# A decoder step on one core: cached keys, values and decays gathered by row number, eight (values: four) consecutive rows of a page to a partition

## The chip, the core and the metric

The kernel runs on one core of one Trainium2 chip. The metric is the device time of one execution in microseconds (us). The text calls the engines PE (TensorE), DVE (VectorE), ACT (ScalarE), POOL (GpSimd) and SP (SyncE). SP computes nothing here; it issues most of the DMAs.

## What is computed

One step of a one-layer decoder: 256 prompt tokens and 8 samples of one token each go through a projection, two kinds of attention beside each other, a gated merge and a mixture of 32 experts. The samples attend to 1024 cached rows each, which lie in 8 pages of 128 rows. Cut to the part that the change touches (all numbers are float32):

```
# cache_k, cache_v (1, 80, 128, 8, 64), cache_logf (1, 80, 128, 8), page_table (8, 8) int32
k_past = cache_k[0][page_table]          # (8 samples, 1024 rows, 8 heads, 64), v_past likewise
suffix = cumsum(logf_past, axis=1, reverse=True) - logf_past      # decays of all later rows
s = einsum('bqhd,bshd->bhqs', q, k_all) * 64 ** -0.5 + cum_new[query] + suffix[key]
o = einsum('bhqs,bshd->bqhd', softmax(s), v_all)
# later: x = x + gate1 * (mix of both attentions) @ w_o;  x = x + gate2 * moe(norm(x))
# moe: top 4 of 32 experts, w_gu (32, 1024, 2048), w_d (32, 1024, 1024)
```

## The kernel before

The program is written out by hand, engine by engine, with semaphores between them. Its first part (about a quarter of the time) holds the projections of the input, the attention of the prompt and of the samples, and the merge. Its second part goes through the experts, four at a time.

**The ring.** Weights, keys and values pass through six slots of 2 MB each. A table (`RING`) lists the items in order of loading, each with its slot: `ada0` to `ada11` (modulation weights), `qa ka va fqk vb rb ga0 ga1 gb0 gb1` (columns of the input projection), `K0` to `K7` (the keys of one sample each), `V0` to `V7` (values), `state`, `wb`, `wo`. SP walks through the table and, for each item, waits until the item before it in that slot has been used. The experts' weights follow, over the same slots and some more homes.

**Keys and values.** An item `K` or `V` is loaded page by page: 128 rows of a page lie on the 128 partitions, 2 KB each, and one DMA of 256 KB brings one page (`load_pages`). The page's number is read from `pages_row` into a register first. SP issues the first four pages of an item, POOL the last four (`second_half`). `K0` holds the eight pages of sample 0, and so on; `V0` holds two pages each of samples 0 to 3, `V1` the next two, and so on, `V4` to `V7` the same for samples 4 to 7.

**Keys on DVE.** `keys_half(b, part)` multiplies four pages of keys by the sample's query, which is the same on every partition, and reduces over the 64 features. The 16 calls stand in DVE's program among the small work of the prompt. The queries of samples 0 and 1 reach all partitions through PE and ACT. Those of samples 2 to 7 go from `q_rows` to DRAM (`q_dram`) and back as three broadcasts (`q_all1` to `q_all3`), all on POOL's queue.

**Decays.** One gather (`lf_rows`) brings the 64 pages' decays with one page on a partition. PE turns them with eight transposes (`past_lf`). A product with ones gives the sum of each page (`page_sums`), a product with a strict triangle the suffix inside a page (`in_page_suffix`). DVE adds up the later pages and gets `past_bias`.

**The prompt's attention.** It runs over the steps s = 0 to 10 on PE, with one head behind another: `pair_scores` fills two banks for two heads, DVE masks (`head_mask`) and normalizes (`head_norm`), ACT takes the exponentials, PE turns the probabilities (`head_turn`) and multiplies by the values (`head_values`). Among these stand tiles of the gates, modulation weights, and `cached_values(i)`: eight products of the samples' probabilities with the item `V{i}`. A bank is used again when DVE has taken what it held (`vector_bank`). A slot is free again when `release` says so.

Of the kernel before, what the change touches and what calls it, by code (L numbers as in the profile page):

```python
# [26 lines left out]
I32 = mybir.dt.int32  # L27
U32 = mybir.dt.uint32
# [15 lines left out]
PAGES, PAGE, N_PHYS = 8, 128, 80  # L44
NE, TOPK, FF = 32, 4, 1024
# [49 lines left out]
def decoder_step(nc, x_prompt, x_sample, c_prompt, c_sample, cache_k, cache_v, cache_logf, state_gla,  # L95
# [4 lines left out]
    with ExitStack() as ctx:  # L100
# [21 lines left out]
        pages_row = sb("pages_row", [1, NS * PAGES], I32)  # L122
        pages_col = sb("pages_col", [NS * PAGES, 1], I32)
# [48 lines left out]
        past_lf = tok[:, 0, 0:512].rearrange("p (a j) -> p a j", j=PAGES)  # L172
# [33 lines left out]
        lf_rows = gla_S[0:NS * PAGES, :, :, :].rearrange("p a b c -> p (a b c)")  # L206
# [52 lines left out]
        q_shift = dec_max[:, 0:36].rearrange("p (i c) -> p i c", c=9)  # L259
        dec_diag = tiny(HA * NS, HA * NS)  # L260
        dec_inv = tiny(P, HA, NS)
# [64 lines left out]
        for item in ITEMS:  # L326
            s = SLOT_OF[item]
            slot_count[s] += 16 * (PAGES // 2 if item[0] in "KV" else 2 if item in WIN else 1)
            landing[item] = (s, slot_count[s])
# [10 lines left out]
        def arrived(eng, item):  # L340
            eng.wait_ge(landed[landing[item][0]], landing[item][1])
# [18 lines left out]
        def page_of(item, n):  # L360

            i = int(item[1:])
            return (i, n) if item[0] == "K" else (4 * (i // 4) + n % 4, 2 * (i % 4) + n // 4)

        def second_half_landed(item):

            i = int(item[1:])
            again = i >= 4 and item != "K7"
            return sig(f"second_half_{item[0]}{i - 4 if again else i}"), 16 * (PAGES // 2) * (2 if again else 1)

        def load_pages(eng, item, half, done, slot_free):

            slot = landing[item][0]
            rows = (cache_k if item[0] == "K" else cache_v)[0].rearrange("n s h d -> n s (h d)")
            order = range(half * PAGES // 2, (half + 1) * PAGES // 2)
            at_ = [b * PAGES + j for b, j in (page_of(item, n) for n in order)]
            pages = [eng.value_load(pages_row[0:1, a:a + 1], min_val=0, max_val=N_PHYS - 1) for a in at_]
            eng.wait_ge(*slot_free)
            for j, page in zip(order, pages):
                eng.dma_start(ring[:, slot, j * WA:(j + 1) * WA],  # L380
# [2300 lines left out]
```

## Time and profile before

| | us |
|---|---|
| median of 3 runs | 1247.59 |
| lowest and highest | 1246.07, 1248.51 |
| span of the profiled execution | 1245.7 |
| PE busy in it | 1167.0 |
| DVE busy | 335.1 |
| ACT busy | 174.9 |
| POOL busy | 48.3 |

The profile shows one execution, from its first instruction to its last; its own time is this span of 1245.7 us, and the median of the runs is 1.9 us above it. In it 500.76 MB were moved at a mean of 402 GB/s. Busy shares are means over parts of the program with different limits, so what matters is read stretch by stretch: which engine is full there, and what ended the waits of the engine that carries the end. Rows of the timeline give start, duration, engine, line, operation and tiles, and in brackets how long the engine had been idle and what released it.

### The profile page before, as it was taken

Reading aid. Unit: us, or ns where it says so; the run is one execution under the profiler, and the core shown is the slowest. Engines: PE = TensorE matmul, PEld = TensorE weight load, DVE = VectorE, ACT = ScalarE, POOL = GpSimd, SP = SyncE. Lnnn points to the kernel's source line nnn. Section 1 sums busy time; section 2 is a strip of 40 time slices with the busy share of each in tenths; the row PEclk is TensorE's granted clock in tenths of the full one; section 3 lists DMA queues with packets and bytes.
Section 4 is the critical chain, followed back from the end, with each engine's and each line's share of the span. In section 5 each row is a group of like instructions: output and inputs, shape, how many; then the busy total and the mean of one; then the engine's idle time right before and its main releaser. Section 6 shows DMA issues by size and latency. Waiting matters only on the chain.

```text
span 1245.7 us, 15295 instructions
## 1 busy us (share of the span) xinstructions
PE 1167.0 (94%) x6044; PEld 587.2 (47%) x6044; DVE 335.1 (27%) x688; ACT 174.9 (14%) x346; POOL 48.3 (4%) x95
## 2 busy tenths in 40 slices
PE   6999999999999999989899979998989989899997
PEld 4788756688543442424243435344332424243333
DVE  3389975523221030111101111111021011103123
ACT  3133232100211100200020011002000200020102
POOL 1132122000000000000000000000000000000000
PEclk9999999999999999999999998999999999999999
DMA  9998999998799999999999999999999999999995
GB/s 341 357 388 314 379 347 383 404 408 345 292 407 429 428 428 427 427 429 428 429 429 417 428 428 411 429 427 428 428 428 427 428 427 429 429 427 427 422 417 204
DMA packets 72700, 500.76 MB, mean 402 GB/s; under 512 B 9049, under 2 KB 11171, under 8 KB 43836
## 3 DMA queue, kind: packets, MB, share of 16 engines
q1 hardware_dynamic: 65840, 478.38, 93.2%
q0 software_dynamic: 6576, 21.42, 4.7%
q8 instruction: 42, 0.69, 0.2%
q14 instruction: 22, 0.18, 0.0%
q10 hardware_dynamic: 220, 0.09, 0.0%
HBM read 496.48 MB, written 3.38 MB: 401 GB/s over the span
## 4 chain that ended last, share of the span: by engine, by line
PE 66%; DMA 25%; SPq 4%; ACT 2%; DVE 2%; issue 2%; DVEq 0%
PE ps L1076 22%; DMA ring<-in_w_d 16%; PE ps L1163 11%; PE ps L518 11%; DMA early<-in_w_d 8%; PE ps L1260 4%; PE ps L1017 4%; PE ps L862 2%; PE ps L927 2%; SPq L2526 2%; PE ps L423 2%; PE ps L960 1%; DMA ring<-in_w_ada 1%; PE ps L475 1%; SPq L2410 1%
## 5 line engine op out<-in xcount | busy, mean ns | idle before, releaser
L1076 PE MATMUL ps<-ring,zone 128*64 128x512 f32 x1488 | 414.9, 593 | 6.0 <-DMA ring<-in_w_gu 3.4
L1163 PE MATMUL ps<-ring,oT 128*64 128x512 f32 x784 | 239.5, 620 | 28.9 <-DMA ring<-in_w_d 15.1
L1076 PEld LDWEIGHTS ps<-ring,zone 128*64 128x64 f32 x1488 | 132.3, 137 | 220.6 <-issue 217.5
L518 PE MATMUL ps<-early,ring 128*128 128x264 f32 x640 | 149.0, 389 | 1.8 <-DVE early L1735 1.4
L2189 DVE TENSOR_SCALAR zone<-ps 128x1024 f32<-128x1024 f32 x14 | 17.1, 1225 | 480.2 <-PE ps L1076 457.8
L1163 PEld LDWEIGHTS ps<-ring,oT 128*64 128x64 f32 x784 | 73.2, 142 | 149.8 <-issue 129.6
L518 PEld LDWEIGHTS ps<-early,ring 128*128 128x128 f32 x640 | 119.5, 190 | 30.2 <-issue 8.9
L1076 PE MATMUL ps<-zone 128*64 128x512 f32 x284 | 114.9, 594 | 2.1 <-DMA ring<-in_w_gu 2.1
L1076 PE MATMUL ps<-early,zone 128*64 128x512 f32 x240 | 98.8, 593 | 0.0
L1547 ACT ACTIVATE ps<-zone 128x1024 f32<-128x1024 f32 x14 | 14.4, 1027 | 452.7 <-DVE zone L2189 452.7
L1076 PEld LDWEIGHTS ps<-zone 128*64 128x64 f32 x284 | 35.2, 137 | 77.7 <-issue 73.8
L2201 DVE TENSOR_TENSOR dec_scores<-dec_scores,ps 128x8 f32<-128x8 f32 x80 | 12.9, 162 | 209.8 <-PE ps L1260 113.4
L1163 PE MATMUL ps<-zone,oT 128*64 128x512 f32 x112 | 52.8, 627 | 11.6 <-DMA ring<-in_w_d 11.6
L1163 PE MATMUL ps<-early,oT 128*64 128x512 f32 x128 | 61.5, 637 | 0.0
L1017 PE MATMUL ps<-zone,early 128*128 128x224 f32 x224 | 44.2, 355 | 0.1
L1017 PEld LDWEIGHTS ps<-zone,early 128*128 128x128 f32 x224 | 41.8, 190 | 0.5
L423 PE MATMUL ps<-ident,zone 128*128 128x128 f32 (+4 forms) x214 | 35.1, 288 | 3.9 <-ACT oT L1570 3.9
L423 PEld LDWEIGHTS ps<-ident,zone 128*128 128x128 f32 (+4 forms) x214 | 26.4, 178 | 25.4 <-issue 20.3
L2202 DVE SCALAR_TENSOR_TENSOR xT<-ps,modT,xT 128x256 f32<-128x256 f32 x80 | 38.1, 478 | 0.0
L1163 PEld LDWEIGHTS ps<-zone,oT 128*64 128x64 f32 x112 | 15.5, 144 | 46.9 <-issue 35.1
L1767 DVE TENSOR_REDUCE dec_scores<-ring 128x32 f32<-128x2048 f32 x16 | 36.6, 2288 | 0.6
L1260 PE MATMUL ps<-zone,gla_S 128*128 128x264 f32 x112 | 33.9, 390 | 1.2 <-ACT oT L1570 0.6
(408 smaller groups left out, 978.8 us busy)
## 6 DMA issues: line engine op xcount, KB each, us to landing
ring<-in_w_gu SPq DMA_DIRECT2D x93, 2048.0 KB, 27.0
ring<-in_w_d SPq DMA_DIRECT2D x45, 2048.0 KB, 22.4
zone<-in_w_gu SPq DMA_DIRECT2D x16, 2048.0 KB, 25.3
early<-in_w_gu SPq DMA_DIRECT2D x15, 2048.0 KB, 30.0
ring<-in_w_ada SPq DMA_DIRECT2D x12, 2048.0 KB, 13.1
ring<-in_w_in SPq DMA_DIRECT2D x18, 1024.0 KB, 12.2
early<-in_w_d SPq DMA_DIRECT2D x8, 2048.0 KB, 24.8
zone<-in_w_d SPq DMA_DIRECT2D x7, 2048.0 KB, 19.5
```

Of the source, the lines that this page charges most:

```text
L423: return pe.transpose(out, in_, ident[0:n, 0:n])
L518: ins = pe.matmul(bank[0:width, 0:T], w[:, k, c0:c0 + width], hT[:, k, :], start=(k == 0), stop=(k == KT - 1))
L862: ins = pe.matmul(bank[:, 0:T], wb[n][:, k, m * P:(m + 1) * P], (oT[:, :, :], obT)[n][:, k, :], start=(k == 0), stop=(k == 3))
L927: ins = pe.matmul(bank[:, 0:T], wo[m // 4][:, k, feature_columns(m % 4)], hT[:, k, :], start=(k == 0), stop=(k == KT - 1))
L1017: ins = pe.matmul(bank[:, kk * 4 * PCAP:(kk + 1) * 4 * PCAP], tok[:, t, k * P:(k + 1) * P], pick[:, t, :, :].rearrange("p e s -> p (e s)") ...
L1076: ins = pe.matmul(ps[64 * j:64 * j + CAP, c, :], xg[:, k, 2 * par + j, :], rows, start=False, stop=(k == KT - 1), skip_group_check=True)
L1163: ins = pe.matmul(ps[64 * j:64 * j + CAP, 4 + c, :], hidT[:, k, j * CAP:(j + 1) * CAP], w[j][:, kk, c * 512:(c + 1) * 512], start=(k == 0) ...
L1260: ins = pe.matmul(ps[:, 6 + m % 2, 0:T], ye_tok[par][:, feature_columns(m)], putT[:, par, :], start=(par == pars[0]), stop=(par == 1))
L1767: V.tensor_reduce(dec_scores[:, b:HA * NS:NS, part_no * n:(part_no + 1) * n] .rearrange("p h j -> p j h"), kc.rearrange("p j (h d) -> p j ...
L2189: V.tensor_scalar(hid, sig_ps, LIMIT, None, ALU.min).then_inc(sig("gate_ready"), 1)
L2202: return V.scalar_tensor_tensor(out=xT[:, m, 0:TP], in0=bank[:, 0:TP], scalar=modT[:, 40 + m, 0:1], in1=xT[:, m, 0:TP], op0=ALU.mult, op1= ...
L2526: sp.dma_start(places[slot][:, kk * D:(kk + 1) * D], dn_last[2 * (PAIRS - 1) + j, 2 * s_ + kk // 2, :, kk % 2, :])\
```

## The change

Rows are addressed by number. A page has 128 rows, so eight consecutive rows of a page lie on one partition: partition p holds rows 8r to 8r + 7 of page j, with j = p // 16 and r = p % 16. The numbers are computed on the chip: a product of the page numbers with a 0/1 matrix on PE, and three small operations on DVE. POOL then issues the gathers: eight for the decays, one of 2 MB for each `K`, two of 1 MB for each `V` (a `V` item now holds four consecutive rows for each of two samples). SP loads no keys and no values any more, and the register reads are gone.

`K0` now waits for the second half of `qa` (`qa_second`) where POOL's half of it waited for `ka`. The other gathers stand where the second halves stood in POOL's program.

With eight consecutive rows on a partition, the suffix inside a partition is added up first on DVE (six adds), and one product with the triangle over the 64 totals gives the rest (`later_rows`). The transposes and the two products over 512 columns go.

`cached_values(i)` takes two items at once, 16 products, each time the four samples after each other. The calls stand at other places: `V0` and `V1` in step 6 where they stood in steps 5 and at the head of 6; `V2` and `V3` in step 8 where they stood in 7 and 8; `V4` and `V5` behind the first part of the linear attention's states; `V6` and `V7` before its third head.

```
-        pages_row = sb("pages_row", [1, NS * PAGES], I32)
-        pages_col = sb("pages_col", [NS * PAGES, 1], I32)
+        rows_at = sb("rows_at", [P, NS], I32)
+        half_rows_at = sb("half_rows_at", [P, 2, NS], I32)
...
-        lf_rows = gla_S[0:NS * PAGES, :, :, :].rearrange("p a b c -> p (a b c)")
+        lf_rows = gla_S[:, :, :, :].rearrange("p a b c -> p (a b c)")[:, 0:NS * RUN * HA]
+        page_of_row = part(attn_flat, slice(0, PAGES), 1024, P)
...
+            pe.wait_ge(sig("row_numbers"), 3)
+            pe.wait_ge(sig("page_rows"), 1)
+            bank = vector_bank()
+            vector_filled(pe.matmul(bank[:, 0:NS], page_of_row, pages_f, start=True, stop=True), "rows_at")
...
-            pe.wait_ge(sig("lf_rows"), 16)
-            bank = vector_bank()
-            for h in range(HA):
-                ins = transpose(bank[:, h * 64:(h + 1) * 64], lf_rows[:, h:h + HA * (PAGE - 1) + 1:HA])
-            vector_filled(ins, "past_lf")
...
+            pe.wait_ge(sig("lf_total"), 1)
             bank = vector_bank()
-            vector_filled(pe.matmul(bank[:, :], ones[:, :], past_lf.rearrange("p a b -> p (a b)"),
-                                    start=True, stop=True), "page_sums")
-            tiles("fqk", 256, "kb", [1])
-            bank = vector_bank()
-            vector_filled(pe.matmul(bank[:, :], after[:, :], past_lf.rearrange("p a b -> p (a b)"),
-                                    start=True, stop=True), "in_page_suffix")
+            vector_filled(pe.matmul(bank[:, 0:HA * NS], after[:, :], lf_total, start=True, stop=True), "later_rows")
...
             def cached_values(i):
-                item, group = f"V{i}", i // 4
-                arrived(pe, item)
-                pe.wait_ge(*second_half_landed(item))
+                items, group = (f"V{i}", f"V{i + 1}"), i // 4
+                for item in items:
+                    arrived(pe, item)
...
-                if s == 6:
-                    cached_values(1)
...
-                elif s in (5, 7, 8):
-                    cached_values(s - 5)
+                elif s in (6, 8):
+                    cached_values(s - 6)
...
-                cached_values(4 + i)
-            cached_values(6)
+                if i == 0:
+                    cached_values(4)
...
                 if h == 2:
-                    cached_values(7)
+                    cached_values(6)
...
+            dve.wait_ge(sig("lf_rows"), 16 * NS)
+            by_head = past_suffix.rearrange("p (h b) j -> p h b j", b=NS)
+            lf = lf_rows.rearrange("p (b j h) -> p h b j", b=NS, h=HA)
+            V.memset(past_suffix[:, :, RUN - 1], 0.0)
+            chain(V.tensor_copy(by_head[:, :, :, RUN - 2], lf[:, :, :, RUN - 1]))
+            for j in range(RUN - 3, -1, -1):
+                chain(V.tensor_tensor(by_head[:, :, :, j], by_head[:, :, :, j + 1], lf[:, :, :, j + 1], ALU.add))
...
+            pool.wait_ge(sig("page_rows"), 3)
+            for b in range(NS):
+                gather_rows(lf_rows[:, b * RUN * HA:(b + 1) * RUN * HA], lf_runs, rows_at[:, b:b + 1], sig("lf_rows"))
...
+                pool.wait_ge(*freed[slot_before(f"K{b}")])
+                gather_rows(ring[:, s, :], k_runs, rows_at[:, b:b + 1], gathered(f"K{b}")[0])
...
-            arrived(pool, "ka")
-            second_half("K0")
+            pool.wait_ge(sig("qa_second"), 32)
+            load_keys(0)
             pool.wait_ge(vector_free, v_index["q_rows"])
             nc.gpsimd.dma_start(q_dram, q_rows).then_inc(sig("q_stored"), 16)
             pool.wait_ge(sig("q_stored"), 16)
...
             for b in range(1, NS):
-                second_half(f"K{b}")
+                load_keys(b)
```

POOL's program before, from the first gather on (L2605 the decays, L380 the second half of `K0`, L2615 and L2618 the queries out and back; the ISA rows set registers):

```order
L2605 DMA gla_S<-in_cache_logf,pages_col 64x1024
L377 TENSOR_LOAD pages_row
...
L380 DMA ring<-in_cache_k 128x512
L380 ISA
L380 DMA ring<-in_cache_k 128x512
L2615 DMA q_dram<-zone 8x512
L2618 DMA early<-q_dram 128x1024 x2
L2618 DMA oT<-q_dram 128x1024
L377 TENSOR_LOAD pages_row
```

And POOL's program after the change, at the same place (L2604 is every gather: decays, keys, values):

```order
L2604 DMA gla_S<-in_cache_logf,rows_at 128x64 x8
L2604 DMA ring<-in_cache_k,rows_at 128x4096
L2630 DMA q_dram<-zone 8x512
L2633 DMA early<-q_dram 128x1024 x2
L2633 DMA oT<-q_dram 128x1024
L2604 DMA ring<-in_cache_k,rows_at 128x4096 x7
L2638 DMA vb_dram<-rows 8x512
L2604 DMA ring<-in_cache_v,half_rows_at 128x2048 x8
```

All of `K1` now stands behind the queries' way to DRAM and back, and eight gathers stand ahead of `K0`.

PE's program before, in steps 5 and 6 (L742 the samples' sums, L712 the cached values, L423 turning probabilities, L688 to L690 values of the prompt, L662 and L666 the scores of heads 6 and 7):

```order
L742 MATMUL ps<-dec_scores,ones 128x512
L712 MATMUL ps<-ring,dec_scores 8x512 x8
L423 MATMUL ps<-ident,attn 128x128 x3
...
L690 MATMUL ps<-attn,v_tok 64x128
L712 MATMUL ps<-ring,dec_scores 8x512 x8
L662 MATMUL ps<-zone 128x128 x2
L666 MATMUL ps<-early,ident 128x128 x2
L662 MATMUL ps<-zone 128x256 x2
L666 MATMUL ps<-early,ident 128x256 x2
L423 MATMUL ps<-ident,attn 128x128 x3
```

And after the change (L732, L703, L418, L680, L652 and L656 are the same lines of code in this order):

```order
L732 MATMUL ps<-dec_scores,ones 128x512
L418 MATMUL ps<-ident,attn 128x128 x3
...
L680 MATMUL ps<-attn,v_tok 64x128
L652 MATMUL ps<-zone 128x128 x2
L656 MATMUL ps<-early,ident 128x128 x2
L652 MATMUL ps<-zone 128x256 x2
L656 MATMUL ps<-early,ident 128x256 x2
L703 MATMUL ps<-ring,dec_scores 8x512 x16
L418 MATMUL ps<-ident,attn 128x128 x3
```

Both sets of eight products, which stood ahead of the scores of heads 6 and 7, now stand behind them.

## Rows read from the trace of the kernel before

**Rows 1.** The page: span, and busy time of TensorE.

```profile
span 1245.7 us, 15295 instructions
...
PE 1167.0 (94%) x6044; PEld 587.2 (47%) x6044; DVE 335.1 (27%) x688; ACT 174.9 (14%) x346; POOL 48.3 (4%) x95
```

**Rows 2.** Stretches: length, busy us of PE, PEld, DVE, ACT, POOL; clock, DMA share, GB/s.

```profile
330.00:340.00 10.00, 10.00 (x50) 3.41 (x48) 0.00 (x0) 0.00 (x0) 0.00 (x0) 1.00 0.70 274
...
400.00:1200.00 800.00, 742.06 (x3531) 307.58 (x3529) 116.32 (x250) 76.73 (x143) 0.50 (x1) 0.98 1.01 426
```

**Rows 3.** The chain that ended last, in the experts: start, us, what.

```profile
599.72 26.74 DMA ring<-in_w_d
```

**Rows 4.** Timeline of DVE, among the keys.

```profile
66.08 2.27 DVE L1766 TENSOR_TENSOR ring<-ring,early 128x2048 f32<-128x2048 f32 x1
...
76.05 2.29 DVE L1766 TENSOR_TENSOR ring<-ring,early 128x2048 f32<-128x2048 f32 x1 [1.13 <-DMA ring<-in_cache_k]
...
82.02 0.71 DVE L1811 TENSOR_TENSOR zone<-zone 128x528 f32<-128x528 f32 x1 [1.35 <-ACT zone L1353]
...
90.49 0.68 DVE L1860 COPY early<-ps 128x512 f32<-128x512 f32 x1
...
102.08 1.83 DVE L1875 TENSOR_TENSOR early<-early 128x64 f32<-128x64 f32 x6
```

**Rows 5.** Timelines of DVE and PE at the first probabilities of the prompt.

```profile
153.05 0.35 DVE L1927 TENSOR_SCALAR attn<-attn,small 128x256 f32<-128x256 f32 x1
...
153.55 0.55 PE L423 MATMUL ps<-ident,attn 128*128 128x128 f32 x3
```

**Rows 6.** Timeline of PE: the decays' transposes and first product.

```profile
81.14 1.09 PE L423 MATMUL ps<-ident,gla_S 64*128 64x64 f32 x8
...
95.85 1.02 PE L631 MATMUL ps<-early,ones 128*128 128x512 f32 x2
```

**Rows 7.** Timeline of POOL: the gather of decays, the first two broadcasts.

```profile
10.90 1.10 POOL L2605 DMA_INDIRECT gla_S<-in_cache_logf,pages_col  x1 [7.77 <-DMA pages_col<-in_page_table]
...
61.87 1.08 POOL L2618 DMA_DIRECT2D early<-q_dram  x2 [5.55 <-DMA q_dram<-zone]
```

**Rows 8.** DMA queues: 65 to 80 us (two rows), then q0, 65 to 67.9.

```profile
q0 software_dynamic: 1076, 3.68, 64.2%
q1 hardware_dynamic: 1117, 2.13, 38.7%
...
q0 software_dynamic: 300, 1.11, 98.4%
```

**Rows 9.** Timelines of PE and SP up to ka; DMA views: issue to landing.

```profile
17.66 0.58 PE L423 MATMUL ps<-ident,zone 36*128 36x36 f32 x3
...
19.39 1.41 SPq L2399 DMA_DIRECT2D ring<-in_w_ada  x1
...
ring<-in_w_ada SPq DMA_DIRECT2D x1, 2048.0 KB, 17.0
...
36.94 1.93 PE L450 MATMUL ps<-ring,early 128*32 128x256 f32 x32
...
22.31 4.89 SPq L2415 DMA_DIRECT2D ring<-in_w_in  x1
...
ring<-in_w_in SPq DMA_DIRECT2D x1, 1024.0 KB, 19.5
...
44.65 2.05 PE L518 MATMUL ps<-early,ring 128*128 128x264 f32 x8
```

**Rows 10.** Timelines of DVE and PE in the prompt's attention and behind it.

```profile
165.17 0.35 DVE L1912 SCALAR_TENSOR_TENSOR attn<-ps,f_tok,early 128x128 f32<-128x128 f32 x1 [1.08 <-PE ps L666]
...
168.26 1.91 PE L712 MATMUL ps<-ring,dec_scores 128*8 128x512 f32 x16
...
174.43 0.49 PE L662 MATMUL ps<-zone 64*128 64x128 f32 x4 [0.86 <-DVE small L1962]
...
204.28 1.09 PE L799 MATMUL ps<-early 64*64 64x128 f32 x16 [0.93 <-DVE gla_S L2003]
```

More of the change, by code:

```diff
@@ L340, in arrived @@
         def arrived(eng, item):
-            eng.wait_ge(landed[landing[item][0]], landing[item][1])
+            eng.wait_ge(*(gathered(item) if item[0] in "KV" else (landed[landing[item][0]], landing[item][1])))
         def gate_up_done(n, first, gone):
@@ L358, in expert_load, with gathered, values_in @@
             return q * 24 + at_, slot, (q * 3 + (at_ // PLACES + 1)) * 16 + slot_count[slot]
-        def page_of(item, n):
-            i = int(item[1:])
[L363 to L380, printed above, removed]
-                              rows[bass.ds(page, 1), :, :].rearrange("a s c -> (a s) c")).then_inc(done, 16)
+        def gathered(item):
+            s, _ = landing[item]
+            before_ = [other for other in ITEMS[:ITEMS.index(item) + 1] if other[0] in "KV" and landing[other][0] == s]
+            return sig(f"gathered{s}"), sum(16 if other[0] == "K" else 32 for other in before_)
+        def values_in(item):
+            i = int(item[1:])
+            return [4 * (i // 4) + 2 * (i % 2) + n for n in range(2)], (i % 4) // 2
         block = ctx.enter_context(nc.Block())
@@ L1324, in _ @@
             dma(c_rows[1:9, :], c_sample, "c_rows")
+            with nc.allow_non_contiguous_dma(reason="64 page numbers"):
+                dma(pages_sb[:, :], page_table.rearrange("b j -> j b"), "pages")
             vectors = {"b_ada": b_ada, "g_mix": g_mix, "g_ffn": g_ffn, "g_gla": g_gla, "b_alpha": b_alpha}
@@ L2387, in load @@
                 earlier = slot_before(item)
-                if item[0] not in "KV" and earlier is not None:
+                if item[0] in "KV":
+                    return
+                if earlier is not None:
                     sp.wait_ge(*freed[earlier])
@@ L2614, in _, with load_values @@
+            def load_values(i):
+                s, _ = landing[f"V{i}"]
+                samples, half = values_in(f"V{i}")
+                pool.wait_ge(*freed[slot_before(f"V{i}")])
+                for n, b in enumerate(samples):
+                    gather_rows(ring[:, s, n * 2048:(n + 1) * 2048], v_runs, half_rows_at[:, half, b:b + 1],
+                                gathered(f"V{i}")[0])
+            pool.wait_ge(sig("qa_second"), 32)
+            load_keys(0)
             pool.wait_ge(vector_free, v_index["q_rows"])
```

97 lines of the change are left out of this document (53 added, 44 removed).

## The prediction

> **What bounds the kernel now.** I read the page first. The span is 1245.7 us and TensorE (PE) is busy for 94% of it [rows 1]. Then I read stretches of the span for who is full. From 400 to 1200 us the DMA engines are full (share 1.01, 426 GB/s) while PE is busy for only 742 of 800 us [rows 2], and the chain shows why: PE stands until a slice of w_d, issued when its slot came free, has landed 26.74 us later [rows 3]. So the last 900 us are DMA-bound. But this DMA stream does not start full. Between 330 and 340 us the engines are only 0.70 busy with PE at 10.00 of 10 us [rows 2]: every slot holds a weight, and the stream waits for PE to use one. So the end is the moment at which PE reaches the experts, plus a stretch that the change doesn't touch. A microsecond won or lost by PE before 330 us is one won or lost at the end; one won by the DMA alone before that is lost in the gap at 330.
>
> The change lies before 220 us. There PE is nearly always busy, and its partner is VectorE (DVE), which works through 16 half samples of keys: per half a multiply of 2.27 us and a reduction that is about as long [rows 4]. The reader is to see in rows 4 that this queue has almost no slack from 66 us on: it waits 1.13 us for the second half of K1 and 1.35 us for ScalarE. All of it stands before the prompt's attention. At the first probabilities DVE ends at 153.40 and PE turns them at 153.55 [rows 5]: 0.15 us of slack. So a late DVE is passed on to PE, and an early PE alone gains little.
>
> **What it removes.** PE loses the eight transposes of the decays (1.09 us) and two products over 512 columns (1.02 us as shown for one) [rows 6], and gets two small ones: some 2.5 us off PE. DVE loses two copies (0.68 each), the add and the second add over 512 elements (about the same each), keeps six adds (1.83) and gets one pass over 512 elements and four small operations: 4.5 us become about 3.3, 1.2 off [rows 4].
>
> **K1 comes late.** Before, half of K1 was issued by SP, ahead of DVE's need, and only the other half by GpSimd. Now all keys are on GpSimd's queue, and K1 stands behind the wait for the stored queries and behind three broadcasts. The first two are issued at 61.87 [rows 7], the third right behind them; the queue then has 3 x 0.52 + 2.10 = 3.67 MB to move before K1 is complete. Bounds: alone on the engines this queue moved 1.11 MB in 2.9 us, 383 GB/s, which gives 9.6 us, so 74 us at the earliest; with the vb weights beside it, it moved just 3.68 MB from 65 to 80 us [rows 8], so 79.5 us. I take 77, between them: vb is still loaded beside it, but SP's K2 half is not. DVE asks for K1 at 66.08, so it stands 10.9 us in place of the 1.13 it stood in the middle of K1; the 1.35 us wait for ScalarE is swallowed, and 1.2 us of work is gone: 10.9 - 1.1 - 1.35 - 1.2 = 7.3 us late (bounds 4.3 and 9.8). What is queued behind: the products and the decay of the prompt, which PE asks for later and gets in time, and the sum over decays, for which PE will stand some us near the place of its 95.85 product [rows 6]; PE then still arrives before DVE at the first probabilities. K2 to K7 are ahead of their use: their slots are free one sample (9.1 us of DVE) earlier than they are needed.
>
> **K0 comes too early.** It now waits for the second half of qa, which SP issues ahead of ada3, and not for ka. Ahead of it are eight gathers of decays. The one gather in the trace took GpSimd 1.10 us for 64 rows [rows 7]. The row numbers come from a product that stands ahead of PE's 17.66 transposes [rows 9]; eight gathers from some 19 us on end at 28 us at the earliest. So K0's 2.10 MB (5.4 us at 389 GB/s) go out beside ada3, issued 19.39 and landed 17.0 us later at 36.4, which PE reads at 36.94, and beside ka, issued 22.31 and landed 19.5 us later at 41.8, which PE reads at 44.65 [rows 9]. ka moves to 47.2, 2.6 us after PE's need; ada3 by 0 to 5 us, by when K0 starts. Bounds 0 (gathers so slow that K0 goes behind ka) and 5.4; I take 2.6. q_rows, and with it K1, moves by the same.
>
> How the queues share matters here. From 65 to 80 us GpSimd's queue had 64.2% of the engines' time and SP's 38.7% [rows 8], each with small packets. The Trainium skill (DMA: Bandwidth & Descriptors, Queues, rings and completion order) says that an engine goes round-robin between its queues packet by packet; larger packets in the gathers would then give them more than that, K1 nearer to 74 and ada3 later. The two nearly cancel, and the trace has no gather of such rows; the sum stays with the shares of the rows.
>
> **The values move behind a wait.** V0 stood in step 5 and V1 at the head of step 6, each 1.91 us of PE (3.7 for both, as neighbours overlap a little); behind them PE stood 0.86 us until DVE released a bank for the next scores at 174.43. DVE got there along its own chain: from 165.17, where it had waited 1.08 us for PE, it did not stand for PE again [rows 10]. Now both stand behind those scores. The wait grows by 3.7 us, and from 174.43 to 190 PE has no other wait in which the 3.7 us could be done. So +3.7 us. Bounds: 0, if DVE were also earlier there by as much; 3.7. I take 3.7. Later V5 moves to before the wait of 0.93 us at 204.28 [rows 10] and fills it: -0.9.
>
> **Sum.** DVE late 7.3, K0 2.6, slack at 153.5 us -0.15, values +3.7 - 0.9 = +12.5 us. PE's own 2.5 us are not in it: PE waits for DVE there. 1245.7 + 12.5 = 1258.2 for an execution like the profiled one; the median of the runs (1247.59) is 1.9 above that span, so 1260. With the low bounds of K1 and K0: 4.3 + 0 - 0.15 + 2.8 = +6.9, 1254.5. With the high ones: 9.8 + 5.4 + 2.65 = +17.8, 1265.5.
>
> **Rivals.**
> 1. As above, 1254.5 to 1265.5: 0.58.
> 2. Only the values cost (1250): K1 lands by 70 us, which needs its 3.67 MB in 6 us, more than any stretch of the trace moved, or DVE's order hides it. 0.12.
> 3. Faster, and the mechanism is the DMA. The caches are 33.5 MB. At the 389 GB/s of 65 to 80 us they take 86.2 us, at the 426 GB/s of the experts' stretch 78.7 [rows 2, 8]; the 7.5 us come off the end if up to 330 us PE is paced by landings: 1240. Against it: the gap at 330 us, and that PE's waits in rows 5 and 10 are for DVE. It decides if PE's stands for landings before 330 us are over 7 us. 0.08. The Trainium skill (DMA: Bandwidth & Descriptors, Measured) speaks for this one: it asks for DMAs of 1 MiB or more, with 341 GB/s at 1 MB and 425 at 16 MB, and the old pieces are 256 KB. By that rule alone the change should be a gain.
> 4. No measurable change (1245 to 1250): PE's 2.5 us come through because K1 is early, and the values' wait shrinks with it. 0.07.
> 5. Much slower (1266 to 1280): a gather of 128 rows costs GpSimd several times 1.10 us or blocks while its queue drains. V4 to V7 are eight gathers, and between PE's work near 174.43, behind which the first of their slots comes free, and its use of values next to 204.28 lie 30 us [rows 10]. It decides from some 4 us a gather; at 5 they last 40 us, 10 us more: 1270. 0.15.
>
> **How the numbers follow.** A measurement of this kernel tells about 0.2% (2.5 us) from no change. Faster is case 3 and the lower edge of case 4: 0.10. Same is the rest of case 4 and a third of case 2: 0.09. Slower is the rest: 0.81. The range 1249 to 1266 leaves out case 3, most of case 4 and case 5 above 1266: a little over 2 in 10 at most. Case 1's own range is 1254.5 to 1265.5.
>
> **What would show it.** In the changed kernel's timeline of DVE: a wait of some 11 us for K1 ahead of the third multiply of keys (it starts near 79 us), the keys finished some 9 us later than before, and no other wait for keys. On PE: a wait for ada3 or ka before 50 us, of 2 to 5 us in all; a wait for the sum over decays near 100 us; a wait of some 4.5 us ahead of the scores of heads 6 and 7. The DMA gap before the experts is there and wider. The prediction is wrong if K1 lands before 72 us, if K0's start lies behind ka's landing, if a gather occupies GpSimd for 3 us or more, or if the experts start at the same time as before.

## The result and the profile after

The changed kernel takes 1260.02 us (median of 4 runs, 1258.69 to 1261.86), the kernel before 1248.03 us in the same comparison (4 runs, 1246.07 to 1248.51). The ratio is 1.0101, 95% interval 1.0079 to 1.0124: slower by 1%, which is 12.6 us by the ratio and 12.0 by the two medians. The profiled execution of the changed kernel has a span of 1256.9 us, 11.2 above that of [rows 1].

The page of the changed kernel: span, busy time, queues, and the chain that ended last.

```profile
span 1256.9 us, 14539 instructions
PE 1169.6 (93%) x6036; PEld 589.5 (47%) x6036; DVE 334.2 (27%) x693; ACT 174.8 (14%) x346; POOL 49.7 (4%) x65
...
q1 hardware_dynamic: 56624, 461.60, 88.6%
q0 software_dynamic: 5088, 38.19, 7.7%
...
PE 59%; DMA 27%; DVE 7%; issue 3%; SPq 2%; ACT 2%; POOL 0%; DVEq 0%
```

The last line is the chain; in the kernel before it reads:

```profile
PE 66%; DMA 25%; SPq 4%; ACT 2%; DVE 2%; issue 2%; DVEq 0%
```

The reader is to see that the busy times hardly say "slower". No engine has more than 3 us more to do than in [rows 1], and there are 756 instructions fewer. Only the chain gives a hint: DVE carries 7% of it and carried 2% before. What changed is when things arrive, so the timelines have to be read.

The changed kernel's timeline of GpSimd (start, us, instruction, idle before and its releaser), from the decays to the third gather of keys:

```profile
19.32 1.15 POOL L2604 DMA_INDIRECT gla_S<-in_cache_logf,rows_at  x1 [15.62 <-DVE half_rows_at L1704]
...
28.30 0.94 POOL L2604 DMA_INDIRECT gla_S<-in_cache_logf,rows_at  x1 [0.30 <-issue]
29.55 0.94 POOL L2604 DMA_INDIRECT ring<-in_cache_k,rows_at  x1 [0.30 <-issue]
```

Most gathers of 128 rows cost GpSimd 0.94 us, whether a row is one of decays or one of keys (16 KB); single ones in this timeline took longer, up to 2.74 us (at 107.17 us). K0 goes out at 29.55 us, as forecast. Its 2 MB run beside ada3, and PE waits for ada3. The changed kernel's timeline of PE in the opening:

```profile
19.70 3.39 PE L445 MATMUL ps<-ring,early 128*32 128x256 f32 x32
...
40.86 3.42 PE L445 MATMUL ps<-ring,early 128*32 128x256 f32 x32 [2.39 <-DMA ring<-in_w_ada]
```

Two things stand in the second row: the wait for ada3 (2.39 us), and 3.42 us for 32 matmuls that took 1.93 before [rows 9]. The granted clock explains the second. Stretches of the changed kernel (columns as in [rows 2]):

```profile
36.00:40.00 4.00, 2.46 (x12) 1.75 (x10) 0.00 (x0) 0.39 (x1) 0.00 (x0) 1.00 1.00 416
40.60:43.80 3.20, 2.94 (x28) 1.38 (x32) 0.00 (x0) 0.00 (x0) 0.00 (x0) 0.50 1.05 388
...
160.20:166.60 6.40, 6.09 (x25) 4.42 (x26) 4.35 (x17) 2.02 (x8) 0.08 (x1) 0.50 1.01 422
...
184.00:187.20 3.20, 3.02 (x20) 2.25 (x24) 1.69 (x7) 0.00 (x0) 1.21 (x2) 0.50 0.02 7
```

A clock of 0.50 is the 1.2 GHz level. It stands right behind each of the three longer waits of PE (2.39, 2.72 and 4.16 us). Up to 350 us the kernel before has one such stretch (3.4 us, at 323 us), the changed one has four, of 17 us in all (at 20.0, 40.5, 160.0 and 183.9 us). The first of these four, and the one of the kernel before, stand behind no wait.

The changed kernel's timeline of DVE at K1 and at the last keys; the first is the multiply that stands at 66.08 in [rows 4], where it had no wait:

```profile
77.53 2.29 DVE L1763 TENSOR_TENSOR ring<-ring,early 128x2048 f32<-128x2048 f32 x1 [5.98 <-DMA ring<-in_cache_k,rows_at]
...
151.59 2.29 DVE L1764 TENSOR_REDUCE dec_scores<-ring 128x32 f32<-128x2048 f32 x1
```

And the changed kernel's timeline of PE at the sum over decays, the first probabilities, and the scores of heads 6 and 7 (the last two answer to the rows at 153.55 and 174.43 in [rows 5, 10]):

```profile
103.90 0.33 PE L626 MATMUL ps<-small,after 128*128 128x64 f32 x2
...
160.51 0.90 PE L418 MATMUL ps<-ident,attn 128*128 128x128 f32 x3 [2.72 <-DVE attn L1923]
...
184.18 0.80 PE L652 MATMUL ps<-zone 64*128 64x128 f32 x4 [4.16 <-DVE small L1958]
```

Two stretches of the changed kernel: the DMA gap before the experts (its place has moved with PE by one slice), and the experts.

```profile
340.00:350.00 10.00, 10.00 (x51) 3.61 (x51) 0.00 (x0) 1.73 (x5) 0.00 (x0) 1.00 0.74 276
...
400.00:1200.00 800.00, 742.04 (x3543) 308.92 (x3541) 118.11 (x243) 78.75 (x146) 0.50 (x1) 0.98 1.01 427
```

**Where the time goes.** I read in both traces when PE starts at the same places of the program. The table is my own, worked out from the start times.

| PE starts | before | after | later by |
|---|---|---|---|
| the product behind ada3 (q's shift) | 42.79 | 48.19 | 5.4 |
| scores of heads 0, 1 | 146.32 | 149.46 | 3.1 |
| scores of heads 2, 3 (behind the first probabilities) | 154.19 | 161.35 | 7.2 |
| scores of heads 6, 7 | 174.43 | 184.18 | 9.8 |
| the transposes behind the attention | 190.72 | 204.97 | 14.3 |
| the new rows, behind the last values | 223.19 | 236.95 | 13.8 |
| the experts | 328.29 | 340.42 | 12.1 |

So there are three places: the opening (+5.4), the first probabilities (+4.0) with a stretch at 1.2 GHz behind them (+2.6), and the values behind the scores (+4.5). Between the first two PE's own saving shows (-2.3). The values' wait of 4.16 us stands ahead of the scores of heads 6 and 7, but two sets of products left the same stretch, so the two cancel there; the cost shows one row further down, where the products now stand.

How much of this is the clock can be read off the same rows. The matmuls in the four stretches took 1.46, 1.49, 2.8 and 1.35 us more than the same ones before, 7.1 in all, and the stretch at 323 us had cost the kernel before 1.6. So about 5.5 of the 12.1 us are the clock, and 6.6 are waits and work.

### The profile page after: what moved, and what is told of

It reads as the page before. It is cut to its first block, busy times and chain, and to the rows that moved or that the text cites. A ratio compares the mean times of both kernels' runs of the same rounds, so it can differ in the third digit from the quotient of the medians.

```text
span 1256.9 us, 14539 instructions
## 1 busy us (share of the span) xinstructions
PE 1169.6 (93%) x6036; PEld 589.5 (47%) x6036; DVE 334.2 (27%) x693; ACT 174.8 (14%) x346; POOL 49.7 (4%) x65
## 4 chain that ended last, share of the span: by engine, by line
PE 59%; DMA 27%; DVE 7%; issue 3%; SPq 2%; ACT 2%; POOL 0%; DVEq 0%
PE ps L1066 23%; DMA ring<-in_w_d 16%; PE ps L1153 11%; DMA early<-in_w_d 8%; PE ps L517 4%; PE ps L1250 4%; PE ps L1007 4%; DVE ring L1763 3%; PE ps L852 2%; PE ps L917 2%; DMA ring<-in_w_ada 2%; DVE dec_scores L1764 1%; PE ps L418 1%; PE ps L950 1%; SPq L2407 1%
## 5 line engine op out<-in xcount | busy, mean ns | idle before, releaser
L2185 DVE TENSOR_SCALAR zone<-ps 128x1024 f32<-128x1024 f32 x14 | 17.1, 1224 | 479.4 <-PE ps L1066 457.0
L418 PE MATMUL ps<-ident,zone 128*128 128x128 f32 (+4 forms) x214 | 35.1, 288 | 3.9 <-ACT oT L1560 3.9
L418 PEld LDWEIGHTS ps<-ident,zone 128*128 128x128 f32 (+4 forms) x214 | 26.4, 178 | 24.8 <-issue 19.8
## 6 DMA issues: line engine op xcount, KB each, us to landing
ring<-in_w_ada SPq DMA_DIRECT2D x12, 2048.0 KB, 13.8
ring<-in_w_in SPq DMA_DIRECT2D x18, 1024.0 KB, 11.8
zone<-in_w_d SPq DMA_DIRECT2D x7, 2048.0 KB, 19.5
```

The costliest lines, as they stand in the source:

```text
L418: return pe.transpose(out, in_, ident[0:n, 0:n])
L2185: V.tensor_scalar(hid, sig_ps, LIMIT, None, ALU.min).then_inc(sig("gate_ready"), 1)
```

## The experiments

Each kernel ran in 5 rounds beside the kernel before. Ratios are those to the kernel before, with the 95% interval. Experiments 1 to 4 ran on one chip, 5 to 7 on a second, 8 and 9 on a third, 10 and 11 on a fourth. The reading of experiments 5 to 11 needs this.

**1. Values back ahead of the scores.** In the loop over steps s of the attention of the changed kernel, with the second group left behind them:

```diff
+                if s == 6:
+                    cached_values(0)
...
-                elif s in (6, 8):
-                    cached_values(s - 6)
+                elif s == 8:
+                    cached_values(2)
```

Each call works through two loads of values, so the first call is V0 and V1.

> The changed kernel, but both V0 and V1 are multiplied ahead of the scores of heads 6 and 7 (where V1 stood before the change). Theory 1 (PE waits there for DVE, and the values only fill the wait): the wait of 4.16 us shrinks to under 1 us, its stretch at half clock goes with it, and the end comes 3.7 to 4.5 us earlier than with the whole change: 1255.5 to 1256.5 us, 1.006 to 1.0068 of before. Theory 2 (the time went to the DMA queues, or to the form of the products, four samples after each other): the place does not matter, 1260 us, 1.010.

1254.2 us (1248.39 to 1259.5), ratio 1.0053 (1.0036 to 1.0069): 5.8 us below the changed kernel. The kernel's timeline of PE at the scores of heads 6 and 7:

```profile
180.53 0.49 PE L652 MATMUL ps<-zone 64*128 64x128 f32 x4 [0.61 <-DVE small L1960]
```

The wait of 4.16 us is 0.61, and the four matmuls take 0.49 us, not 0.80: the stretch at 1.2 GHz is gone with the wait. The size is less sure than the mechanism: the 12 runs spread over 11 us, the profiled one took 1250.68, and it differs from the changed kernel in more than this place. The wait for ada3 was 4.32 us in it, with 6.8 us at 1.2 GHz, and behind the first probabilities (a wait of 1.95 us) the clock did not fall.

**2. K0 behind ka again.**

```diff
-            pool.wait_ge(sig("qa_second"), 32)
+            arrived(pool, "ka")
             load_keys(0)
```

> The changed kernel, but the gather of K0 waits for ka, as the old second half did, and not for the second half of qa. Theory 1 (K0 beside ada3 costs PE a wait of 2.39 us and 1.5 us of half clock): no wait for ada3, ada3 and ka land before 37 and 43 us, q_rows 4 us earlier, K1 lands near 73.5 in place of 77.5 us, and the end comes some 4 us earlier: 1256 us, 1.0065. Theory 2 (the small gathers of decays ahead of K0 slow ada3, not K0): ada3 still lands at 39 us or later, and the end moves by under 1 us.

1257.0 us (1255.56 to 1258.71), ratio 1.0076 (1.0058 to 1.0094). No wait for ada3 is left, and PE reaches the product behind it at 44.34 us, 3.9 us earlier, although the stretch at 20 us is there too. The interval overlaps that of the changed kernel, so it is the trace and not the ratio that shows this gain. DVE's wait for K1 is still there (timeline of DVE, then of PE at the first probabilities):

```profile
72.83 2.29 DVE L1763 TENSOR_TENSOR ring<-ring,early 128x2048 f32<-128x2048 f32 x1 [5.13 <-DMA ring<-in_cache_k,rows_at]
```

```profile
155.81 0.55 PE L418 MATMUL ps<-ident,attn 128*128 128x128 f32 x3 [2.72 <-DVE attn L1923]
```

**3. K1 right behind K0, ahead of the wait for the queries.** On top of experiment 2:

```diff
             load_keys(0)
+            load_keys(1)
             pool.wait_ge(vector_free, v_index["q_rows"])
...
-            for b in range(1, NS):
+            for b in range(2, NS):
                 load_keys(b)
```

> As the kernel with K0 behind ka, and K1 gathered right behind K0, ahead of the wait for the queries. Theory 1 (K1 behind the queries' way to DRAM and back makes DVE late, and DVE passes that on to PE at the first probabilities): DVE's wait of 5.98 us for K1 is gone, the keys are finished at 146 us or earlier in place of 153.9, PE's wait of 2.72 us for the first probabilities is under 1 us, and the end comes another 5 to 6 us earlier than with K0 behind ka alone: 1250 to 1251 us, 1.002. Theory 2 (K1 only looks late because DVE is free; PE sets the time up to 150 us): the end moves by under 1.5 us against that kernel.

1250.71 us (1248.92 to 1257.85), ratio 1.0037 (1.0022 to 1.0052). DVE no longer waits for K1; it waits 2.57 us for ScalarE where it waited 1.35 before [rows 4], and ends its keys at 144.99 us, 1.9 us earlier than the kernel before. PE's wait at the first probabilities is 0.33 us. The wait at the scores of heads 6 and 7 is untouched (timeline of PE):

```profile
151.53 0.55 PE L418 MATMUL ps<-ident,attn 128*128 128x128 f32 x3 [0.33 <-DVE attn L1923]
...
172.51 0.49 PE L652 MATMUL ps<-zone 64*128 64x128 f32 x4 [4.16 <-DVE small L1958]
```

**4. The kernel before, with its values at the changed kernel's places.** Nothing else of the change.

```diff
-                if s == 6:
-                    cached_values(1)
...
-                elif s in (5, 7, 8):
+                elif s in (6, 8):
+                    cached_values(s - 6)
                     cached_values(s - 5)
...
-                cached_values(4 + i)
-            cached_values(6)
+                if i == 0:
+                    cached_values(4)
+                    cached_values(5)
...
+                    cached_values(6)
```

> The kernel before, with page loads and all, only the products with the values stand at the changed kernel's places: items V0 and V1 behind the scores of heads 6 and 7, V2 and V3 together in step 8, V4 and V5 behind the first part of the states, V6 and V7 before the third head. Theory 1: PE waits 3.7 us longer ahead of those scores (0.86 becomes 4.5), gets 0.9 back later and loses up to 1.7 us at half clock: 1251 to 1252.5 us, 1.0025 to 1.0035. Theory 2 (place doesn't matter): 1248, 1.000.

1253.44 us (1252.83 to 1253.95), ratio 1.0047 (1.0031 to 1.0063), about 5.9 us for one move in the order of PE's work, some more than expected. The timeline of PE has the same wait as the changed kernel, in a kernel without any gather of keys (behind it 6.8 us at 1.2 GHz, and 3.4 more from 224.6 us on):

```profile
174.31 0.80 PE L662 MATMUL ps<-zone 64*128 64x128 f32 x4 [4.16 <-DVE small L1963]
```

**5. Experiments 1 and 3 together.**

> The changed kernel with K0 behind ka, K1 gathered right behind K0, and V0 and V1 multiplied ahead of the scores of heads 6 and 7. Theory 1 (the three places carry the whole loss, each in its own way, and they add up): PE's waits for DVE ahead of the first probabilities and of the scores are under 1 us each; against the kernel with the first two alone (1250.7) the 4 to 5 us of the values come off: 1246 to 1247.5 us, 0.9985 to 0.9995 of before. Theory 2 (a part of the loss lies in the gathers themselves, by their traffic or by GpSimd): it stays above 1249.5 us, 1.0015 or more.

A miss: 1251.28 us (1249.91 to 1253.79), ratio 1.0033 (1.002 to 1.0047). The waits at the probabilities and at the scores are small, as expected (0.35 and 0.61 us). But this execution lost 4.9 us against experiment 3 in the opening. The timelines of ScalarE and of PE there, and a stretch:

```profile
23.94 0.38 ACT L1368 ACTIVATE rows<-ps 128x256 f32<-128x256 f32 x1 [9.61 <-remote]
```

```profile
24.37 0.70 PE L418 MATMUL ps<-ident,rows 128*128 128x128 f32 x2 [2.38 <-ACT rows L1368]
```

```profile
24.40:31.00 6.60, 5.20 (x12) 3.82 (x13) 1.97 (x7) 1.71 (x4) 4.02 (x5) 0.50 1.03 387
```

PE had ended the product that ScalarE copies at 21.99 us, and ScalarE started 1.95 us after it. "remote" means that the trace can't say what released it. Behind that wait PE runs at 1.2 GHz for 6.8 us.

**6. Other DVE work put into the wait for K1.** In the changed kernel the three steps behind the first half of K1 (the new products and the decay of the prompt) go ahead of it:

```diff
-            keys_half(1, 0)
...
+            keys_half(1, 0)
```

> The changed kernel, only DVE's order differs: the products of the new keys and the decay's first part (4.2 us of work) stand ahead of K1's first half and not behind it. Theory 1 (DVE's queue is what carries K1's delay): that work runs inside the wait for K1, the keys are finished some 4 us earlier (near 150 us), PE's wait for the first probabilities (2.72 us) goes, and the end comes 3 to 5 us earlier: 1255 to 1257 us, 1.006 to 1.0075. Theory 2 (PE's late start of 5.4 us, from ada3, sets the time, and DVE hides behind it): under 1 us earlier, since PE's own start is unchanged.

A miss as well: 1263.89 us (1259.8 to 1265.26), ratio 1.0137 (1.0121 to 1.0154). The moved work waits itself, 3.39 us for PE and 1.22 us for ScalarE, because it uses what PE only then makes; the last keys are reduced from 150.75 us, only 0.84 earlier. And the opening had the same late copy (ScalarE at 24.74 us) with 6.8 us at 1.2 GHz, so this time can't be put down to the moved work alone.

**7. The kernel before with 2.1 MB more to move.** GpSimd's queue copies 2.1 MB of keys inside DRAM near 221 us.

```diff
+            nc.gpsimd.dma_start(extra_dram, cache_k[0, 0:8].rearrange("n s h d -> (n s) (h d)"))\
+                .then_inc(sig("extra"), 16)
```

> The kernel before, with one DMA more: GpSimd copies 2.1 MB of keys to an unused place in DRAM near 221 us, when the DMA engines are full and before the gap at 330 us. Theory 1 (the DMA stream has slack before 330 us; there it waits for PE): the gap gets smaller by about the 5.4 us that 2.1 MB take at 389 GB/s, and the time stays within 1 us of before, 0.999 to 1.001. Theory 2 (bytes before 330 us count at the end, so fewer or cheaper ones would be a gain): 5 us slower, 1.004.

1247.98 us (1244.71 to 1251.64), ratio 1.001 (0.9999 to 1.0022), as expected. Two stretches of the kernel with the extra copy, and then one of them in the kernel before:

```profile
310.00:320.00 10.00, 10.00 (x77) 8.40 (x80) 4.80 (x26) 3.67 (x7) 0.00 (x0) 1.00 0.75 293
330.00:340.00 10.00, 10.00 (x50) 3.34 (x48) 0.00 (x0) 0.00 (x0) 0.00 (x0) 1.00 0.85 339
```

```profile
310.00:320.00 10.00, 10.00 (x77) 8.27 (x79) 4.98 (x27) 3.84 (x7) 0.00 (x0) 1.00 0.49 188
```

The extra traffic fills the gap before the experts (0.49 to 0.75, and 0.70 [rows 2] to 0.85) and costs 0.22% at the upper end of the interval. So DMA time that the gathers save or cost before 330 us is worth next to nothing here by itself.

**8 and 9. The decays' gathers behind K0 and K1.** They are the one burst on GpSimd's queue during the late copy of experiment 5. Experiment 8 is experiment 5 with this edit, experiment 9 is experiment 3 with it:

```diff
-            for b in range(NS):
-                gather_rows(lf_rows[:, b * RUN * HA:(b + 1) * RUN * HA], lf_runs, rows_at[:, b:b + 1], sig("lf_rows"))
...
             load_keys(0)
             load_keys(1)
+            for b in range(NS):
+                gather_rows(lf_rows[:, b * RUN * HA:(b + 1) * RUN * HA], lf_runs, rows_at[:, b:b + 1], sig("lf_rows"))
```

> The kernel with all three (the first two gathers of keys back to back behind the arrival of ka, both first gathers of values ahead of the scores), and the eight gathers of the decays moved behind those two gathers of keys, to about 44 us; nothing else. Before, ScalarE's copy of the modulation rows started at 23.94 us with all three together and at 21.2 to 21.5 in the kernels where only one thing was moved, while eight issues of GpSimd for the decays ran from 19 to 29 us. Theory A: that traffic of GpSimd's queue is what delayed the copy (and through it TensorE, with 6.8 us at 1.2 GHz and 4.9 us lost by the product with q); with it gone TensorE stands at the shifted scores at 42.5 us, not 47.5, and the time is 5 us lower, 1245.5 to 1247. Theory B: the copy waits for something else that has nothing to do with those gathers; it still starts near 24 us and the time stays at 1250 to 1252. The decays are wanted at about 95 us, and neither theory lets them be late.

> The kernel with the first two gathers of keys behind the arrival of ka, and the eight gathers of the decays moved behind them in the same way; the values stay at the changed kernel's places. Its opening had no delay with the gathers at 19 to 29 us (copy at 21.5 us, TensorE at the shifted scores at 42.6). Theory A: no change but a few tenths, 1250 to 1251, with the wait of 4.16 us at the scores of heads 6 and 7 still there. Theory B: the copy's start goes with the program and not with the gathers, so it can be delayed here too; then 1253 to 1256. Beside the run with the values moved it also measures that move once more: 3.5 to 4.5 us if both openings are alike.

Both miss in time: 1251.31 us (1248.26 to 1255.03), ratio 1.0021 (1.0004 to 1.0037), and 1259.89 us (1251.99 to 1264.73), ratio 1.0084 (1.0062 to 1.0105). But the late starts moved with the gathers. In experiment 8 the gathers are issued from 43.69 to 53.41 us, the copy of the opening is on time (21.97 us), and now ScalarE and DVE are late there (timelines of ScalarE, DVE and PE):

```profile
52.31 0.39 ACT L1338 ACTIVATE zone<-ps 128x264 f32<-128x264 f32 x1 [4.41 <-remote]
```

```profile
54.44 0.31 DVE L1746 TENSOR_REDUCE small<-ps 128x36 f32<-128x144 f32 x1 [8.17 <-remote]
```

```profile
50.20 0.60 PE L418 MATMUL ps<-ident,rows 128*128 128x128 f32 x4
...
56.08 2.05 PE L559 MATMUL ps<-ident,zone 128*128 128x128 f32 x16 [1.73 <-DVE zone L1751]
```

DVE's reduction reads what the row at 50.20 makes. In experiment 3 the same pair stands at 48.15 and 48.79 us, 0.04 us between the end and the start; here it is 3.6. Experiment 9 has the same two late starts (54.33 and 55.07 us) and PE waits 2.12 us. Its profiled execution, the slowest of its 12 runs (two took 1252, the others 1257 to 1265), also ran at 1.2 GHz for 17.1 us from 328 us on; why, the trace doesn't tell. Experiment 9 was also to measure the values' move once more, at 3.5 to 4.5 us: against experiment 8 it is 7.9 us (1.0084 and 1.0021), and how much of that is the values this pair can't tell.

**10 and 11. The gathers of the decays where nothing waits, and experiment 5 once more.** Experiment 10 puts the eight gathers behind the fourth gather of keys; experiment 11 is the kernel of experiment 5, unchanged.

```diff
-            for b in range(2, NS):
+            for b in range(2, 4):
                 load_keys(b)
+            for b in range(NS):
+                gather_rows(lf_rows[:, b * RUN * HA:(b + 1) * RUN * HA], lf_runs, rows_at[:, b:b + 1], sig("lf_rows"))
+            for b in range(4, NS):
+                load_keys(b)
```

> The kernel with all three (first two gathers of keys behind the arrival of ka, both first gathers of values ahead of the scores), and the eight gathers of the decays behind the fourth gather of keys, which puts them at about 72 to 82 us, where GpSimd's queue is otherwise idle and TensorE runs on products that wait for no copy. With them at 19 to 29 us ScalarE's copy came 2 us late in this kernel (23.94 us), with them at 43 to 53 us ScalarE came 1.9 us late at 52.31 and VectorE 3.6 us late at 54.44, each with a release that the trace can't name. Theory A: engines start late while GpSimd works through a row of small gathers, and only then; from 72 to 82 us nothing on the path waits for them, so the opening and the product with q run as before the change: TensorE at the shifted scores at 42.4 to 42.9 us and at the product that makes q_all at 52 to 52.5, span 1243 to 1245, time 1245.5 to 1247.5, level with the kernel before. Theory B: the late starts go with the other changes of this kernel; one shows at 22 to 24 us or at 50 to 55 us again, and the time stays at 1250 to 1252.

> The kernel with all three once more, unchanged, decays' gathers at 19 to 29 us, beside the run with them behind the fourth gather of keys. A second profile tells whether the late copy at 23.94 us is fixed in this program or comes and goes between executions. Theory A (a chance hit while the gathers run): time 1250 to 1252 as before, the late start may be there or not; if it is not, TensorE stands at the shifted scores at 42.5 to 43.5 us and that execution is 4 to 5 us below the one profiled before. Theory B (fixed by the program): late start at 23.9 us again.

1246.8 us (1244.21 to 1251.71), ratio 0.999 (0.9974 to 1.0006), and 1247.14 us (1243.87 to 1250.16), ratio 0.9996 (0.9981 to 1.0012). Both are level with the kernel before. In experiment 11 the copy is on time, with the gathers at 19 to 29 us, as the timeline of PE shows:

```profile
22.23 0.50 PE L418 MATMUL ps<-ident,rows 128*128 128x128 f32 x2 [0.51 <-ACT rows L1368]
24.20 7.36 PE L517 MATMUL ps<-early,ring 128*128 128x264 f32 x32 [1.46 <-DVE early L1736]
```

So the late start is not fixed by the program: the same kernel had it in one profile and not in another, and its ratio was 1.0033 in one comparison and 0.9996 in the other, with intervals that don't meet. The two comparisons ran on different chips, and that is the rival to a chance of the single execution: all four profiles with gathers on the second and third chip have late starts, and none of the five on the first and fourth has. Experiment 10 had no release that the trace can't name, but its position forecast missed: PE stood at the product behind ada3 at 45.94 us, since two stretches at 1.2 GHz (3.4 us each, at 19.5 and 26.3 us) came without a late start. Between the two places for the decays these runs show no difference, but on a chip where neither place had a late start.

## Why the prediction came out as it did

The time, the sign and the three places are as forecast. The sizes are not: the forecast made K1 too dear by 5.7 us on DVE and had no term for the clock, which cost 5.5, and these two cancel.

**The bound.** Right. The end follows the moment at which PE reaches the experts (+12.1 us there, +11.2 at the end), the experts' stretch is unchanged (742.04 us of PE, 1.01, against [rows 2]), and experiment 7 shows by itself that earlier DMA time is swallowed. That takes away rival 3. The gap before the experts is there, but not wider, as was forecast: from 322.1 to 362.1 us the DMA share is 0.80, and at the same place before, from 310 to 350 us, 0.76. The Trainium skill (DMA: Bandwidth & Descriptors, Measured) asks for pieces of 1 MiB and more; the pieces did become large, and no gain at the end came of it, since the stream waits for PE at 330 us.

**K0 too early: forecast 2.6 us, measured 5.4 in the trace.** The 2.6 us stood for a wait for ka. PE has none: the product with ka starts at 50.05 us right behind the one ahead of it. The wait is for ada3, 2.39 us, where the working allowed 0 to 5. What was not in the sum is the clock: the 32 matmuls behind the wait took 1.49 us more, and 1.46 us more were lost in the stretch at 20.0 us. That stretch can't be put down to the gathers: experiments 2, 6 and 10 have one there, and 10 has no gather at that time, while 1, 3, 5 and 11 have none. The product for the row numbers adds 0.55 us, and 0.5 for an earlier load is gone. Undoing this part alone gives 1.0101 to 1.0076, about 3.1 us, and 3.9 us in the trace. In experiment 1, with the same opening, the wait was 4.32 us and PE 6.3 us late at the product behind ada3, so 5.4 is one reading of a cost that varies.

**How the queues share.** This is how K0 holds up ada3. The changed kernel's queues from 35 to 37 and from 37 to 39 us, with K0 in q0 and the weights in q1 (packets, MB, share):

```profile
q0 software_dynamic: 45, 0.74, 87.1%
q1 hardware_dynamic: 48, 0.12, 15.3%
...
q0 software_dynamic: 48, 0.79, 92.8%
q1 hardware_dynamic: 46, 0.10, 12.4%
```

Both queues moved about as many packets, but one of K0 has 16 KB and one of the weights some 2 KB, so the weights got 12 to 15% of the engines' time; from 35 to 39 us in the kernel before they had all of it. The Trainium skill (DMA: Bandwidth & Descriptors, Queues, rings and completion order) has the engines go between queues packet by packet, and these rows agree with it. The kernel before agrees too: from 72 to 74 us its queues moved 146 and 159 packets, with 63.0% and 39.2% of the time, because both kinds were small there. The forecast's sum went by such shares [rows 8]; by the counts, rows of 16 KB nearly stop the weights beside them.

**K1 late: forecast 7.3 us less 0.15 of slack, measured 1.6 us on DVE and 4.4 us on PE.** This is the term that was mis-sized most. DVE ends its keys 7.0 us later than before; 5.4 of these are the opening's, so K1 itself made DVE 1.6 us late. Its mechanism is right: the third multiply waits for K1, at 77.53 us where I had some 79, and experiment 3 removes the wait. But the wait is 5.98 us and not 10.9. K1 landed at 77.5 us with an opening 5.4 us late, that is 72.1 without it, outside my bounds of 74 and 79.5. Of the 4.9 us of error 2.9 are the wait for the stored queries, which was 2.68 us and not 5.55 [rows 7]. The other 2.0 go with the weights beside the keys, which took almost nothing where the forecast had them take their share. The changed kernel's queues from 66.5 to 77.5 us (packets, MB, share):

```profile
q0 software_dynamic: 558, 4.11, 96.0%
q1 hardware_dynamic: 80, 0.16, 3.9%
```

The rest of the difference is small: DVE's work is 1.4 us lighter, not 1.2, and a wait of 0.41 us for PE (at 91.93 us before) is gone, so 5.98 - 1.13 - 1.35 - 0.41 - 1.4 = 1.7 us. On PE this shows as waits of 0.85 and 2.72 us at the first probabilities, against a saving of 2.3. The other 2.8 of PE's 4.4 us are the stretch at 1.2 GHz behind them, which no step had. Undoing K1 gives 1.0076 to 1.0037, about 4.9 us, within one comparison.

**The values: forecast +3.7 - 0.9, measured +4.5 - 0.5 in the trace, about 5.9 by experiment.** The forecast wait of some 4.5 us ahead of the scores of heads 6 and 7 is there, 4.16. The rest is the clock again: behind it PE runs at 1.2 GHz for 3.4 us, which cost 1.35. V5 did fill the wait of 0.93 us [rows 10], but a new one of 0.60 us stands ahead of the new rows. Experiment 4 puts this part alone into the kernel before (+5.9), so the term needs nothing of the rest of the change; experiment 1 takes it out of the changed kernel (-5.8), with the reservations made there.

**A wait for the sum over decays near 100 us.** Wrong: the row at 103.90 has none. DVE was late by less than I took, and PE later.

**GpSimd.** The gathers at 0.94 us each end rival 5.

**How the costs add up.** Inside one comparison, experiment 3 stands at 1.0037 and experiment 4 puts the values at 0.0047, which would leave 0.999 with all three gone (an estimate). Experiment 11 has that kernel at 0.9996, and 10, with the decays elsewhere, at 0.999, so on their chip the layout of the gathers is worth nothing measurable by itself, and the loss is in three placements. On the two other chips 0.33% and 0.21% were left (experiments 5 and 8), with the late starts in the profiles. Step by step the path from 1.0101 to 0.9996 reads 3.1, 4.9 and 5.1 us; its sum of 13.1 is only the distance between its ends, and its first and last step cross comparisons, which are sure to no better than 4 us, as experiments 5 and 11 show.

That the forecast of 12.5 us lies beside 12.1 at the experts and 12.6 by the ratio is luck. Without the clock the same places cost 6.6 us, below the sum's own low bound of 6.9; the clock, in no term of it, brought the other 5.5.

## What to carry to other kernels

When many small loads on two queues become few large ones on one queue, write down for each large one what it now stands behind and what it now runs beside; on one chip the copy itself cost nothing measurable here, its place cost 12 us. What runs beside it suffers by the size of the packets: rows of 16 KB left the weights 12 to 15% of the engines' time. Work of the bottleneck engine that stood ahead of a wait is free cover: moving it behind the wait costs its whole length, and here the clock on top. And cost a wait of PE at more than its length: in the changed kernel waits of 2.4 to 4.2 us were followed by 3.4 to 6.8 us at 1.2 GHz, 1.3 to 2.8 us lost again each time.

## What the runs showed of the hardware

**The clock behind short waits.** After waits of 2.39, 2.72 and 4.16 us PE was granted 1.2 GHz for 3.4, 6.8 and 3.4 us. In experiment 3 the wait of 4.16 us, which ended at 172.51, is followed by 3.4 us from 173.0 on. The length of the wait alone doesn't decide it. The same wait of 4.16 us was followed by 6.8 us in experiment 4, the one of 2.72 by 3.4 in experiment 2; waits of 1.95 (experiment 1), 2.12 (9) and 2.20 us (6) by none. Experiment 10 had 3.4 us at 1.2 GHz from 26.3 us on behind a wait of 1.40, and experiment 11 the full clock behind a wait of 1.46 at the same place.

**Packets, not bytes, are shared between two queues.** Where the gathers' rows of 16 KB ran beside weights, both queues moved about as many packets: 45 and 48 from 35 to 37 us, 48 and 46 from 37 to 39 us. In experiment 2, where K0 goes out later, it is 47 and 44 from 47 to 49 us, with 90.7% and 11.8% of the engines' time.

**Engines that start late while GpSimd gathers.** In four of ten profiles with gathers of keys ScalarE or DVE started late, by up to 4.0 us (51.03 to 55.07 in experiment 9) after the end of what it reads. At eight places the trace can't name the release: at 23.94 us (experiment 5), 24.74 and 206.73 (6), 52.31 and 54.44 (8), 54.33, 55.07 and 202.48 (9). ScalarE's starts at 197.15 (5) and 196.31 us (8) belong to them: it had stood idle for 3.76 and 3.93 us, as at 202.48 and 206.73 (4.43 and 4.40), where it stood 1.85 in all nine other profiles. Each time GpSimd was issuing gathers or had ended its last one less than 2 us before, and moving the decays' gathers from 19 us to 43 us moved the late starts with them. But gathers are not enough: the four profiles are all those with such gathers on the second and third chip, and the six others, on other chips as far as is recorded, have none. The three profiles of kernels without those gathers (the kernel before, experiments 4 and 7) have none either, and experiment 7 ran on the second chip. What is held up is open, and so is what of it is the chip's: only the kernel of experiments 5 and 11 was profiled on two chips.
